# Rows gathered into expert order in the first sixteen blocks, and down weights in 8 KB pieces

## The chip, the cores and the metric

The kernel runs on one core of a Trainium2 chip. The time is the device time of an execution, in microseconds. The engines are TensorE (PE, its weight loads PEld), VectorE (DVE), ScalarE (ACT), GpSimd (POOL) and SyncE (SP, which issues DMAs).

## What is computed

A transformer block over 512 tokens of 1024 columns in float32. Attention and a convolution branch come first; they are not touched except for where their buffers lie. The rest is a mixture of 64 experts:

```python
h = rmsnorm(x, g_ffn)
grp  = argmax(h @ w_rg + b_rg)                       # 1 of 8 groups
top_v, top_j = top_k(le[grp], 2)                     # 2 of 8 experts of the group
wts  = pg_top * softmax(top_v)
y_e  = (silu(h_e @ w_g[e]) * (h_e @ w_u[e])) @ w_d[e]  # rows h_e of the tokens that chose e
x    = rmsnorm(x + sum over both choices of wts * y_e, g_final)
```

Each token has two experts, so there are 1024 rows for 64 experts. An expert has 6 MB of weights: gate and up 1024x512, down 512x1024, in float32.

## The kernel before

The expert stage works in blocks of `BLK` = 64 rows of one expert. The blocks of the first `AHEAD` = 2 experts are blocks 0 and 1; the others are counted at run time (`count_i`, read by every engine as `nblk`; with these inputs 60, 62 blocks in all) and listed in `small_i`, so the loops over blocks are hardware loops.

Weights. The buffer `weights` has 12 places of 1 MB, two sets of six by the block's parity. A set holds gate and up of the first half of the columns (sixths 0, 1), of the second half (2, 3), and down in two halves (4, 5). SP issues a sixth of block b+2 when PE has used that of block b (`gu_used` after each half of gate and up, `down_used` after the block) and when the same sixth of block b+1 has landed (`in_w`), L517 to L525. For gate and up a partition gets 8 KB in one piece; for down two pieces of 4 KB (L476, L485).

Rows. The rows of a block are picked out of `h2` by a product with a one-hot matrix, in every block anew: `gather` (L1378) multiplies, for each of four token tiles, the one-hot of 64 slots with the two halves of `h2`, and sums over the tiles in `ps_rows`. DVE copies them to `rows_sb` (L1120), PE transposes them (`transpose_rows`, L1389), DVE copies them to `hTb` (L1122). The gather for block b+1 stands between the products of block b: tiles 0 and 1 behind the first half of gate and up, tile 2 behind the second half, tile 3 behind the transposes of act, the transposes of rows between the halves of down. DVE makes the one-hot of the next block at the start of a block (L1098 to L1101).

The rest of a block. ACT takes silu of gate (L765), DVE multiplies by up (L1117, `act`), PE transposes act (L1417), ACT copies it (L767), PE multiplies with down (L1426), ACT copies the result to `y_sb` (L773) and GpSimd scatters its rows to `expert_rows` in DRAM (L579). At the end SP reads these rows back (L531), DVE adds them with their weights (L1142) and normalizes.

Before the first block DVE works out the routing in a chain of small operations in which each waits for the one before (`link`); `prepare_slots` (L1061) and `take_slots` (L1075), which list the destination rows of all slots, stand in block 0.

## Time and profile before

| what | us |
|---|---|
| median of 3 runs (1401.35 to 1402.8) | 1401.41 |
| the profiled execution | 1401.0 |
| its span in the trace | 1399.2 |
| PE busy | 1327.6 (95%) |
| DVE busy | 431.9 (31%) |
| ACT busy | 209.4 (15%) |
| GpSimd busy | 186.3 (13%) |
| bytes read from HBM | 429.1 MB |

Times in the views are counted from the start of the span. In the slices of the page each digit is the busy share of 1/40 of the span, 35 us, in tenths. "PEclk" is the clock granted to TensorE. A PE row of the timeline merges instructions of one line; its first number is the start of the first of them, its second reaches to the end of the last, which overlaps the next row. The expert loop fills the span from 430 to 1371 us.

### The profile page before, as it was taken

Reading aid. Unit: us, or ns where it says so; the run is one execution under the profiler, and the core shown is the slowest. Engines: PE = TensorE matmul, PEld = TensorE weight load, DVE = VectorE, ACT = ScalarE, POOL = GpSimd, SP = SyncE. Lnnn points to the kernel's source line nnn. Section 1 sums busy time; section 2 is a strip of 40 time slices with the busy share of each in tenths; the row PEclk is TensorE's granted clock in tenths of the full one; section 3 lists DMA queues with packets and bytes.
Section 4 is the critical chain, followed back from the end, with each engine's and each line's share of the span. In section 5 each row is a group of like instructions: output and inputs, shape, how many; then the busy total and the mean of one; then the engine's idle time right before and its main releaser. Section 6 shows DMA issues by size and latency. Waiting matters only on the chain.

```text
span 1399.2 us, 17476 instructions
## 1 busy us (share of the span) xinstructions
PE 1327.6 (95%) x5883; PEld 580.5 (41%) x5883; DVE 431.9 (31%) x843; ACT 209.4 (15%) x453; POOL 186.3 (13%) x244
## 2 busy tenths in 40 slices
PE   5999988999979999999999999999999999999991
PEld 3878766744453333333333333333333333333330
DVE  4799344342334221121121122122112112112214
ACT  3232324430110100100000000010010000000002
POOL 2355433000000001001001001000100100100100
PEclk9999999999978999999999999999999999999996
DMA  5331311116145999999999999999999999999984
GB/s 208 115 121 61 121 60 57 68 57 251 49 180 219 386 417 416 417 417 417 416 418 417 415 417 417 415 416 417 416 417 417 413 414 410 415 414 415 416 339 186
DMA packets 93090, 435.78 MB, mean 311 GB/s; under 512 B 13488, under 2 KB 13517, under 8 KB 60810
## 3 DMA queue, kind: packets, MB, share of 16 engines
q1 hardware_dynamic: 86896, 429.23, 76.1%
q0 software_dynamic: 5312, 5.28, 1.2%
q10 hardware_dynamic: 858, 0.95, 0.2%
q8 instruction: 15, 0.25, 0.1%
q14 instruction: 9, 0.07, 0.0%
HBM read 429.10 MB, written 18.36 MB: 320 GB/s over the span
## 4 chain that ended last, share of the span: by engine, by line
issue 78%; PE 13%; POOL 2%; DVE 2%; DMA 2%; POOLq 1%; ACT 1%; ACTq 0%; DVEq 0%
PE ps_proj L1193 10%; PE ps_proj L1234 2%; POOL sb_tick L578 1%; POOL sb_tick L589 1%; DVE sb_x L1142 1%; DMA sb_weights<-in_w_in 1%; DMA sb_rb_sb<-in_rel_bias 1%; PE ps_scores L1248 1%; POOL expert_rows L579 0%; DVE sb_x L1152 0%; DVE sb_conv L932 0%; DMA sb_weights<-expert_rows 0%; POOL sb_weights_r L557 0%; PE ps_proj L1216 0%; PE ps_proj L1225 0%
## 5 line engine op out<-in xcount | busy, mean ns | idle before, releaser
L1405 PE MATMUL ps_proj<-sb_weights,sb_scratch 128*64 128x512 f32 x1984 | 446.9, 592 | 0.8 <-DVE sb_scratch L1107 0.8
L1405 PEld LDWEIGHTS ps_proj<-sb_weights,sb_scratch 128*64 128x64 f32 x1984 | 142.3, 137 | 283.2 <-issue 271.8
L1382 PE MATMUL ps_proj<-sb_hT,sb_scratch 128*64 128x512 f32 x1008 | 254.0, 605 | 0.0
L1426 PE MATMUL ps_scores<-sb_weights,sb_scratch 128*64 128x512 f32 x992 | 237.0, 598 | 0.0
L1117 DVE TENSOR_TENSOR sb_scratch<-sb_scratch,ps_proj 128x256 f32<-128x256 f32 x62 | 26.1, 421 | 536.0 <-ACT sb_scratch L765 536.0
L578 POOL TENSOR_TENSOR sb_tick<-sb_tick 1x1 f32<-1x1 f32 x62 | 11.6, 187 | 1013.9 <-ACT sb_scratch L773 1013.9
L1193 PE MATMUL ps_proj<-sb_hT_r,sb_weights_r 128*128 128x512 f32 x512 | 126.9, 401 | 2.7 <-POOL sb_weights_r L557 2.7
L1382 PEld LDWEIGHTS ps_proj<-sb_hT,sb_scratch 128*64 128x64 f32 x1008 | 67.4, 138 | 120.5 <-issue 120.5
L1426 PEld LDWEIGHTS ps_scores<-sb_weights,sb_scratch 128*64 128x64 f32 x992 | 65.3, 136 | 116.9 <-issue 90.3
L1193 PEld LDWEIGHTS ps_proj<-sb_hT_r,sb_weights_r 128*128 128x128 f32 x512 | 96.8, 192 | 30.5 <-issue 10.1
L765 ACT ACTIVATE sb_scratch<-ps_proj 128x256 f32<-128x256 f32 x62 | 23.8, 385 | 492.1 <-PE ps_proj L1405 492.1
L557 POOL TENSOR_TENSOR sb_weights_r<-sb_weights,sb_weights_r 128x1024 fp32r<-128x1024 f32 x36 | 86.0, 2404 | 76.4 <-ACT sb_weights_r L640 75.4
L773 ACT ACTIVATE sb_scratch<-ps_scores 128x512 f32 (+1 forms) x62 | 37.0, 598 | 318.6 <-PE ps_scores L1426 311.0
L1122 DVE COPY sb_scratch<-ps_proj 128x512 f32<-128x512 f32 x62 | 42.9, 692 | 99.5 <-PE ps_proj L1389 99.5
L1120 DVE COPY sb_scratch<-ps_proj 128x512 f32<-128x512 f32 x62 | 42.9, 691 | 96.1 <-PE ps_proj L1382 96.1
L579 POOL DMA_INDIRECT expert_rows<-sb_scratch,sb_idx x62 | 61.4, 991 | 32.3 <-issue 31.9
L1193 PE MATMUL ps_proj<-sb_x_r,sb_weights_r 128*128 128x512 f32 x256 | 63.2, 389 | 0.0
L1341 PE MATMUL ps_proj<-sb_weights 128*128 128x512 f32 x128 | 55.6, 593 | 0.0
L1193 PEld LDWEIGHTS ps_proj<-sb_x_r,sb_weights_r 128*128 128x128 f32 x256 | 48.1, 188 | 10.0
L1389 PEld LDWEIGHTS ps_proj<-sb_consts,sb_scratch 128*128 128x128 f32 x252 | 26.6, 142 | 52.1 <-issue 50.3
L1098 DVE TENSOR_TENSOR sb_scratch<-sb_small,sb_consts 128x512 f32<-128x512 f32 x62 | 43.0, 693 | 7.6 <-issue 1.2
L845 DVE SCALAR_TENSOR_TENSOR ps_scores<-sb_pad,sb_taps,ps_scores 128x512 f32<-128x512 f32 x58 | 42.5, 752 | 0.9
(221 smaller groups left out, 811.1 us busy)
## 6 DMA issues: line engine op xcount, KB each, us to landing
sb_weights<-in_w_exp_down SPq DMA_DIRECT2D x124, 1024.0 KB, 13.8
sb_weights<-in_w_exp_gate SPq DMA_DIRECT2D x124, 1024.0 KB, 14.0
sb_weights<-in_w_exp_up SPq DMA_DIRECT2D x124, 1024.0 KB, 15.2
sb_weights<-in_w_in SPq DMA_DIRECT2D x9, 2048.0 KB, 7.9
sb_x<-in_x SPq DMA_DIRECT2D x8, 512.0 KB, 9.2
sb_weights<-in_w_out SPq DMA_DIRECT2D x2, 2048.0 KB, 10.5
sb_weights<-expert_rows SPq DMA_DIRECT2D x4, 1024.0 KB, 7.9
sb_weights<-in_w_conv_pw SPq DMA_DIRECT2D x1, 2048.0 KB, 7.7
```

Of the source, the lines that this page charges most:

```text
L557: pool.tensor_tensor(w_low[name][:, :, j * P:(j + 1) * P], raw, high.bitcast(F32), ALU.subtract).then_inc(w_split, 1)
L579: pool.indirect_dma_start(out=y_dram, out_offset=bass.IndirectOffsetOnAxis(ap=idx[:, parity:parity + 1], axis=0), in_=y_sb[:, parity, :], ...
L773: act_e.activation(y_sb[:, of_parity(b), :].rearrange("p a s -> p (a s)"), ps_y, ACT.Copy)\
L845: dve.scalar_tensor_tensor(out=dst, in0=pad[:, c, k:k + SEQ], scalar=taps[:, c, k:k + 1], in1=conv_sum[c], op0=ALU.mult, op1=ALU.add).then ...
L1098: dve.tensor_tensor(hot_k, over(dest, BLK), pos8, ALU.is_equal).then_inc(loop_v, 1)
L1120: dve.tensor_copy(rows_sb, ps_rows[:, :]).then_inc(rows_ready, 1)
L1122: dve.tensor_copy(hTb, ps_hTb[:, :].rearrange("p (c s) -> p c s", s=P)).then_inc(hTb_ready, 1)
L1193: last = mm(dst[:, :], w[:, c, :], rows[:, c, :], start=i + c == 0, stop=i == 2 and c == KD - 1)
L1341: last = mm(dst[:, :], gates[:, c, t * P:(t + 1) * P], w[:, c, :], start=c == 0, stop=c == KD - 1)
L1382: last = mm(ps_rows[g * BLK:(g + 1) * BLK, :], onehot[:, t, :], h2[:, t, g * NW:(g + 1) * NW], start=t == 0, stop=t == T - 1)
L1405: last = mm(ps_gu[g * BLK:(g + 1) * BLK, :].rearrange("p (a n) -> p a n", a=2), hTb[:, c, half * BLK:(half + 1) * BLK], weights[:, place(p ...
L1426: last = mm(ps_y[g * BLK:(g + 1) * BLK, :], actT[:, j, half * BLK:(half + 1) * BLK], weights[:, place(parity, 4 + half), 2 * j + g, :], st ...
```

## The change

The rows that a block needs are no longer gathered in every block. 1024 rows fill sixteen blocks of 64, so the rows are gathered sixteen times, in expert order with no gaps, into `hTs`, a buffer that holds them transposed (slot by slot, the eight column chunks of a slot side by side). This is done for the rows of the experts from the third on, beside the blocks 0 to 15; blocks 0 and 1 get their rows as before. Every block from the third on copies its 64 rows from `hTs` to `hTb` (`sorted_to_block`), from a start that DVE reads from `start_i`. `sorted_places`, new on DVE in block 0, works out each row's place and the starts, with two small products on PE (`rest_of_experts`). In the blocks with a gather PE does tiles 2 and 3 between the halves of gate and up, the transposes of rows behind the second half, tile 0 of the next ones behind the transposes of act, tile 1 between the halves of down. Blocks after the sixteenth have no gather and no transposes of rows.

The buffers `v_sb`, `conv`, `strip` and `pad` become parts of one buffer `work`, over which `hTs` and the routing's temporaries lie. A half of down is laid out so that a partition gets two neighbouring rows of the weights, 8 KB in one piece; act is transposed with a stride of two (`act_jf`) to match. The smallest count of loop blocks becomes 16.

```diff
@@ -49,12 +49,15 @@
 BLK = 64
 AHEAD = 2
 MAXB = 80
-MINLOOP = 2 * SEQ // BLK - AHEAD
+MINLOOP = 2 * SEQ // BLK
+GATHERED = 2 * SEQ // BLK - AHEAD
+WORK = 64 + 2 * SEQ * KD + BLK * KD
 NW = 512
 EPS = 1e-6
 LAM_INIT = 0.8 - 0.6 * math.exp(0.0)
 NEG = -3.0e38
 FAR = 1.0e6
...
-        v_sb = sb("v_sb", [P, T, CW])
         scratch = sb("scratch", [P, 4096])
-        pad = sb("pad", [P, KC, SEQ + TAPS - 1])
-        conv = sb("conv", [P, KC, SEQ])
-        strip = sb("strip", [P, HEADS, SEQ])
+        work = sb("work", [P, WORK + 64])
+        v_sb = work[:, 0:2048].rearrange("p (t n) -> p t n", n=CW)
+        conv = work[:, 2048:4096].rearrange("p (c s) -> p c s", s=SEQ)
+        strip = work[:, 4096:6144].rearrange("p (h s) -> p h s", s=SEQ)
+        pad = work[:, 6144:6144 + KC * (SEQ + TAPS - 1)].rearrange("p (c s) -> p c s", s=SEQ + TAPS - 1)
+        hTs = work[:, 128:128 + KD * (2 * SEQ + BLK)]
...
+        act_jf = act.rearrange("p (f j) -> p j f", j=2)
...
-            wd = ap("w_exp_down")[0].rearrange("e (h j p) n -> e h p j n", h=2, p=P)
+            wd = ap("w_exp_down")[0].rearrange("e (h p j) n -> e h p (j n)", h=2, p=P)
...
-                    dst = dst.rearrange("p a (j q) n -> p (a j) (q n)", j=2)
-                    src = wd[e, i - 4].rearrange("e p j n -> (e p) j n")
+                    dst = dst.rearrange("p a b n -> p (a b n)")
+                    src = wd[e, i - 4].rearrange("e p n -> (e p) n")
...
+            def sorted_places():
+                link(dve.tensor_scalar(ecap, const("ahead", NE), float(BLK), ecount, ALU.mult, ALU.min))
+                link(dve.tensor_tensor(erest, ecount, ecap, ALU.subtract))
+                dve.tensor_scalar(erest_b, const("ones", NE), erest, None, ALU.mult).then_inc(rest_ready, 1)
+                link(dve.tensor_tensor(efirst, eend, eblk, ALU.subtract))
+                link(dve.tensor_scalar(efirst, efirst, float(BLK), None, ALU.mult))
+                link(dve.tensor_scalar(starts_m, const("block", NE)[:, 0:MAXB], float(BLK), efirst, ALU.mult, ALU.subtract))
+                link(dve.tensor_scalar(starts_m, starts_m, 0.0, erest, ALU.max, ALU.min))
+                dve.tensor_scalar(starts_m, starts_m, float(KD), None, ALU.mult).then_inc(starts_in, 1)
+                dve.wait_ge(rest_done, 1)
+                link(dve.tensor_copy(cstart, ps_oT[:, 0:NE]))
+                link(dve.tensor_scalar(cstart[:, 0:AHEAD], cstart[:, 0:AHEAD], -float(BLK) - STATIC, None, ALU.add))
+                link(dve.tensor_scalar(over_c, ranks[:, :, 0:AHEAD], float(BLK), STATIC, ALU.is_ge, ALU.mult))
+                link(dve.tensor_tensor(crank, ranks, cstart.unsqueeze(1).to_broadcast([P, T, NE]), ALU.add))
+                link(dve.tensor_tensor(crank[:, :, 0:AHEAD], crank[:, :, 0:AHEAD], over_c, ALU.add))
+                for k in range(2):
+                    link(dve.tensor_tensor(hot_c, hot_e[:, k], crank, ALU.mult))
+                    ins = dve.tensor_reduce(cdest.rearrange("p (t k) -> p t k", k=2)[:, :, k], hot_c, X, ALU.add)
+                    if k == 0:
+                        link(ins)
+                    else:
+                        ins.then_inc(loop_v, 1)
+                dve.wait_ge(starts_done, 1)
+                link(dve.tensor_copy(start_i[0:1, :], ps_t[0:1, 256:256 + MAXB]))
...
+            def block_onehot():
+                dve.wait_ge(loop_v, 2)
+                dve.tensor_tensor(hot_k, over(dest, BLK), pos8, ALU.is_equal).then_inc(loop_v, 1)
+                dve.wait_ge(loop_v, 3)
+                dve.tensor_tensor(onehot, onehot2[:, :, 0, :], onehot2[:, :, 1, :], ALU.add).then_inc(hot_b, 1)
             def next_onehot(before, after):
                 dve.wait_ge(loop_v, before)
...
+                dve.tensor_tensor(hot_k, over(cdest, BLK), pos8, ALU.is_equal).then_inc(loop_v, 1)
                 dve.wait_ge(loop_v, after)
...
+                dve.tensor_scalar(cdest, cdest, -float(BLK), None, ALU.add).then_inc(loop_v, 1)
                 dve.tensor_tensor(onehot, onehot2[:, :, 0, :], onehot2[:, :, 1, :], ALU.add).then_inc(hot_b, 1)
...
+            def copy_rows(n):
+                dve.wait_ge(rows_done, n)
+                dve.tensor_copy(rows_sb, ps_rows[:, :]).then_inc(rows_ready, 1)
+            def rows_to_block(n):
+                dve.wait_ge(hTb_done, n)
+                dve.tensor_copy(hTb, ps_hTb[:, :].rearrange("p (c s) -> p c s", s=P)).then_inc(hTb_ready, 1)
+            def rows_to_sorted(n, at):
+                dve.wait_ge(hTb_done, n)
+                dve.tensor_copy(hTs[:, at].rearrange("p (s g c) -> p c g s", g=2, c=4),
+                                ps_hTb[:, :].rearrange("p (c g s) -> p c g s", c=4, g=2)).then_inc(hTs_ready, 1)
+            def sorted_to_block(start):
+                dve.tensor_copy(hTb.rearrange("p c (g s) -> p c g s", g=2),
+                                hTs[:, bass.ds(start, BLK * KD)].rearrange("p (s g c) -> p c g s", g=2, c=4))\
+                    .then_inc(hTb_ready, 1)
+            def gate_and_up(b):
                 dve.wait_ge(gsig_ready, b + 1)
                 dve.tensor_tensor(act, gsig, ps_gu[:, 256:512], ALU.mult).then_inc(act_ready, 1)
...
+            def list_rows(b, block_slots):
                 if not isinstance(b, int):
                     dve.wait_ge(y_free, b - 1)
                 dve.tensor_copy(idx[:, of_parity(b)], block_slots).then_inc(idx_ready, 1)
...
+            copy_rows(1)
+            rows_to_block(1)
+            dve.wait_ge(rows_done, 1)
+            block_onehot()
+            sorted_places()
+            prepare_slots()
+            gate_and_up(0)
+            copy_rows(2)
+            rows_to_block(2)
+            take_slots()
+            list_rows(0, slots[:, 0:1])
+            def block_with_gather(b, at, start, block_slots):
+                copy_rows(b + 2)
+                next_onehot(2 * b + 4, 2 * b + 5)
+                gate_and_up(b)
+                rows_to_sorted(b + 2, at)
+                dve.wait_ge(hTs_ready, b)
+                sorted_to_block(dve.value_load(start, min_val=0, max_val=2 * SEQ * KD))
+                list_rows(b, block_slots)
+            dve.wait_ge(rows_done, 2)
+            next_onehot(4, 5)
+            block_with_gather(1, slice(0, BLK * KD), start_i[0:1, 0:1], slots[:, 1:2])
             weigh_choices()
             nblk = dve.value_load(count_i[0:1, 0:1], min_val=MINLOOP, max_val=MAXB - AHEAD)
...
+            with dve.Fori(0, GATHERED) as i:
+                block_with_gather(i + AHEAD, bass.ds(BLK * KD * (i + 1), BLK * KD), start_i[0:1, 1:][:, bass.ds(i, 1)],
+                                  slots[:, AHEAD:][:, bass.ds(i, 1)])
+            n = GATHERED + AHEAD
+            copy_rows(n + 2)
+            rows_to_sorted(n + 2, slice(BLK * KD * (n - 1), BLK * KD * n))
+            dve.wait_ge(hTs_ready, n)
+            with dve.Fori(GATHERED, nblk) as i:
+                gate_and_up(i + AHEAD)
+                sorted_to_block(dve.value_load(start_i[0:1, 1:][:, bass.ds(i, 1)], min_val=0, max_val=2 * SEQ * KD))
+                list_rows(i + AHEAD, slots[:, AHEAD:][:, bass.ds(i, 1)])
...
+            def rest_of_experts():
+                pe.wait_ge(rest_ready, 1)
+                mm(ps_oT[:, 0:NE], erest_b, before[0:NE, 0:NE], start=True, stop=True).then_inc(rest_done, 1)
+                pe.wait_ge(starts_in, 1)
+                mm(ps_t[0:1, 256:256 + MAXB], ones[0:NE, 0:1], starts_m, start=True, stop=True).then_inc(starts_done, 1)
+            def gate_up_half(b, parity, half):
+                pe.wait_ge(in_w[2 * half], 16 * b + 16)
+                pe.wait_ge(in_w[2 * half + 1], 16 * b + 16)
+                for c in range(4):
+                    for g in range(2):
+                        last = mm(ps_gu[g * BLK:(g + 1) * BLK, :].rearrange("p (a n) -> p a n", a=2),
+                                  hTb[:, c, half * BLK:(half + 1) * BLK],
+                                  weights[:, place(parity, 2 * half, 2), c, g * 256:(g + 1) * 256],
+                                  start=half + c == 0, stop=half * c == 3)
+                last.then_inc(gu_used, 1)
+            def transpose_act(b):
                 pe.wait_ge(act_ready, b + 1)
                 for c in range(2):
...
+                    last = pe.transpose(ps_actT[:, c * P:(c + 1) * P], act_jf[:, c, :], ident)
                 last.then_inc(actT_done, 1)
...
+            def down_half(b, parity, half):
+                pe.wait_ge(in_w[4 + half], 16 * b + 16)
+                for j in range(2):
+                    for g in range(2):
+                        last = mm(ps_y[g * BLK:(g + 1) * BLK, :], actT[:, j, half * BLK:(half + 1) * BLK],
+                                  weights[:, place(parity, 4 + half), 2 * j + g, :],
+                                  start=half + j == 0, stop=half * j == 1)
+                if half:
+                    last.then_inc(down_used, 1)
+            def first_block():
+                pe.wait_ge(hTb_ready, 1)
+                gate_up_half(0, 0, 0)
+                rest_of_experts()
+                pe.wait_ge(hot_b, 2)
+                gather([0, 1])
+                gate_up_half(0, 0, 1)
+                gather([2])
+                transpose_act(0)
+                gather([3])
+                pe.wait_ge(actT_ready, 1)
+                down_half(0, 0, 0)
+                pe.wait_ge(rows_ready, 2)
+                transpose_rows()
+                down_half(0, 0, 1)
+                slot_rows()
+                pe.wait_ge(hot_b, 3)
+                gather([0, 1])
+            def block_with_gather(b, parity):
+                pe.wait_ge(hTb_ready, b + 1)
+                gate_up_half(b, parity, 0)
+                gather([2, 3])
+                gate_up_half(b, parity, 1)
+                pe.wait_ge(rows_ready, b + 2)
+                transpose_rows()
+                transpose_act(b)
+                pe.wait_ge(hot_b, b + 3)
+                gather([0])
                 pe.wait_ge(actT_ready, b + 1)
...
+                down_half(b, parity, 0)
+                gather([1])
+                down_half(b, parity, 1)
+            def block_products(b, parity):
+                pe.wait_ge(hTb_ready, b + 1)
+                gate_up_half(b, parity, 0)
+                gate_up_half(b, parity, 1)
+                transpose_act(b)
+                pe.wait_ge(actT_ready, b + 1)
+                down_half(b, parity, 0)
+                down_half(b, parity, 1)
+            first_block()
+            block_with_gather(1, 1)
+            with pe.Fori(0, GATHERED // 2) as i:
+                for parity in range(2):
+                    block_with_gather(2 * i + parity + AHEAD, parity)
+            gather([2, 3])
+            pe.wait_ge(rows_ready, GATHERED + AHEAD + 2)
+            transpose_rows()
             pe.wait_ge(listed, 1)
             nblk = pe.value_load(count_i[0:1, 0:1], min_val=MINLOOP, max_val=MAXB - AHEAD)
...
+            with pe.Fori(GATHERED // 2, nblk // 2) as i:
                 for parity in range(2):
                     block_products(2 * i + parity + AHEAD, parity)
             with pe.If((nblk & 1) > 0):
```

## Rows read from the trace of the kernel before

**Rows 1.** Page, part 2: busy tenths of forty slices, granted clock, DMA engines.

```profile
PE   5999988999979999999999999999999999999991
...
PEclk9999999999978999999999999999999999999996
DMA  5331311116145999999999999999999999999984
```

**Rows 2.** Timeline of PE in the loop: start, us, line, operation, count.

```profile
815.80 3.60 PE L1405 MATMUL ps_proj<-sb_weights,sb_scratch 128*64 128x512 f32 x16
819.23 1.03 PE L1382 MATMUL ps_proj<-sb_hT,sb_scratch 128*64 128x512 f32 x4
820.34 0.44 PE L1417 MATMUL ps_aT<-sb_consts,sb_scratch 128*128 128x128 f32 x2
...
821.62 1.89 PE L1426 MATMUL ps_scores<-sb_weights,sb_scratch 128*64 128x512 f32 x8
823.44 0.66 PE L1389 MATMUL ps_proj<-sb_consts,sb_scratch 128*128 128x128 f32 x4
824.03 1.94 PE L1426 MATMUL ps_scores<-sb_weights,sb_scratch 128*64 128x512 f32 x8
```

**Rows 3.** The same timeline of PE in the last block.

```profile
1361.00 3.60 PE L1405 MATMUL ps_proj<-sb_weights,sb_scratch 128*64 128x512 f32 x16
...
1369.22 1.94 PE L1426 MATMUL ps_scores<-sb_weights,sb_scratch 128*64 128x512 f32 x8
```

**Rows 4.** DMA issues of 434.1, 705.0, 780.7, 680 to 695, 1345.1: KB, landing.

```profile
sb_weights<-in_w_exp_gate SPq DMA_DIRECT2D x1, 1024.0 KB, 5.2
...
sb_weights<-in_w_exp_down SPq DMA_DIRECT2D x1, 1024.0 KB, 10.2
...
sb_weights<-in_w_exp_down SPq DMA_DIRECT2D x1, 1024.0 KB, 11.5
...
sb_weights<-in_w_exp_gate SPq DMA_DIRECT2D x2, 1024.0 KB, 11.4
...
sb_weights<-in_w_exp_up SPq DMA_DIRECT2D x1, 1024.0 KB, 15.1
```

**Rows 5.** DMA rates: slices of 700 to 1000; stretches 488:490 and 575:577.

```profile
GB/s 422 414 422 410 421 412 421 412 423 413 418 413 421 411 419 410 424 410 422 411 421 410 419 416 418 414 419 411 422 412 419 414 421 411 418 415 419 416 420 414
...
DMA packets 119, 0.86 MB, mean 430 GB/s; under 512 B 14, under 2 KB 14, under 8 KB 14
...
DMA packets 247, 0.82 MB, mean 408 GB/s; under 512 B 48, under 2 KB 48, under 8 KB 247
```

**Rows 6.** Timeline around the first block: DVE, PE and SP's queue.

```profile
421.66 0.16 DVE L1048 SCALAR_TENSOR_TENSOR sb_conv<-sb_strip,sb_consts 128x2 f32<-128x2 f32 x1
...
424.30 0.42 DVE L1058 TENSOR_REDUCE sb_strip<-sb_conv 128x4 f32<-128x256 f32 x1
...
430.89 0.16 DVE L1064 TENSOR_SCALAR sb_strip<-sb_strip 128x8 f32<-128x8 f32 x1
...
435.54 0.43 DVE L1073 COPY sb_v_sb<-sb_v_sb 128x512 f32<-128x512 f32 x1
439.16 0.42 DVE L1117 TENSOR_TENSOR sb_scratch<-sb_scratch,ps_proj 128x256 f32<-128x256 f32 x1 [3.20 <-ACT sb_scratch L765]
...
445.19 2.01 PE L1375 MATMUL ps_scores<-sb_conv,sb_v_sb 128*128 128x80 f32 x16
447.13 1.08 PE L1405 MATMUL ps_proj<-sb_weights,sb_scratch 128*64 128x512 f32 x4
...
451.34 0.35 SPq L487 DMA_DIRECT2D sb_weights<-in_w_exp_gate  x1
```

**Rows 7.** Timeline of DVE: a strided operation, a copy, and a register load.

```profile
398.02 1.97 DVE L982 SCALAR_TENSOR_TENSOR sb_hT<-sb_x,sb_small,sb_g_ffn 128x1024 f32<-128x1024 f32 x1
...
460.67 0.69 DVE L1122 COPY sb_scratch<-ps_proj 128x512 f32<-128x512 f32 x1 [1.60 <-PE ps_proj L1389]
...
463.57 0.69 DVE L1098 TENSOR_TENSOR sb_scratch<-sb_small,sb_consts 128x512 f32<-128x512 f32 x1 [1.25 <-issue]
```

84 lines of the change are left out of this document (19 added, 65 removed).

## The prediction

> **What bounds the kernel now.** I read the slices of the page first. From the fourteenth slice to the thirty-eighth the PE row is all nines and so is the DMA row [rows 1]: that is the expert loop, 62 blocks, 900 of the 1399 us, with two resources that both look full. A full-looking engine may still be waiting in short pieces, so the next view is the timeline of one block [rows 2]. It shows the order on PE and the starting time of each piece. Half of the gate and up products is 16 products from 815.80 to 819.23, 3.43 us or 0.214 each; a gathered tile is four (0.86), a half of the down products eight (1.71), the transposes of rows take 0.59 (823.44 to 824.03), and those of act with one tile and the wait for their copy 1.28 (820.34 to 821.62), of which 0.05 is wait if the transposes take 0.37. A block has 64 products (13.71), with both kinds of transposes 14.67. From the half that starts at 815.80 to that of the last block at 1361.00 [rows 3] are 36 blocks, so the period is 15.14 and has not moved. The missing 0.47 is four small gaps; the largest, 0.25, stands before the act transposes (819.23 and 0.86 to 820.34). So PE sets the period and hardly ever waits for weights.
>
> The transfers are a hair slower than PE. The time from issue to landing of the first down piece of a block is 10.2 us at 705, 11.5 at 780 (five blocks later); it was 5.2 for the first piece of the loop and is 15.1 for the last up piece [rows 4]. It grows by 0.26 us a block, so the DMA needs 15.14 + 0.26 = 15.40 us for the six pieces of a block while PE needs 15.14, and the lead with which weights land is eaten up. At the end the last up piece is issued at 1345.1 and lands 15.1 later, at 1360.2 [rows 4]; the products that read it start at 1361.00 [rows 3]. PE and DMA reach the end within 1 us of each other. That is the key to this case: take all gathering from PE in 46 of 62 blocks and the DMA stream, whose end does not move for it, takes over at once.
>
> **The gather leaves 46 blocks.** A block then costs PE 3.43 + 3.43 for gate and up, 1.11 until the act transposes (819.23 to 820.34), 1.28 from them to the first down product (820.34 to 821.62; part of that is a gathered tile, so this is an upper value), 3.43 for down: 12.7 us at most against 15.4 of DMA [rows 2]. PE has 2.7 us to spare a block, and 62 x 6 MB still have to come. What this alone gives is the end: after the last up piece lands (1360.2), PE needs 3.43 + 1.11 + 1.28 + 3.43 = 9.25 us, so it ends the products at 1369.4; before, the last half of down starts at 1369.22 and ends 1.71 later, at 1370.93 [rows 3]. Gain 1.5 us. The two down pieces land behind it at 2.6 us each (15.4 for six), before their products come, and are not waited for.
>
> **Down weights as 8 KB pieces.** Two stretches of 2 us hold one size of piece alone: with 8 KB 430 GB/s, with 4 KB 408 [rows 5]. The 2.1 MB of down of a block take 4.88 us at the one rate and 5.14 at the other, 0.26 apart. The row of forty slices of 7.5 us between 700 and 1000 alternates, since a slice is half a block: the slices without down average 420.6 GB/s, those with it 412.2. Down pieces fill about 0.68 of the latter, so they run at 408.2, and 2.1 MB take 5.137 instead of 4.986 us: 0.15 a block [rows 5]. I take 0.15, because that row averages 20 blocks and the two stretches only 2 us each; the bounds are 0.26 above and 0 below (if the slices with down are slower for the row scatters in them). The permutation of rows of act (a transposed operand of stride two) has no row; 0 to 0.1 us on PE, hidden in the late blocks by the 2.7. The new layout of buffers and the clearing of 512 columns on GpSimd stand at the start, where no row shows a wait for GpSimd's first work; I cost them at nothing.
>
> The Trainium skill (DMA: Bandwidth & Descriptors, Specifications) puts the smallest transfer for line rate at 512 B. By it the merged piece brings 0; the two stretches above speak against it, with 430 against 408 GB/s.
>
> **The first block.** The change puts `sorted_places` on DVE between the one-hot and `prepare_slots`, and holds PE for its two products. In the rows of before, the one-hot is just over when `prepare_slots` begins at 430.89; it runs to 435.97, 5.08 us [rows 6]; nothing waits for it, since gate-times-up comes only at 439.16. The new function is about 8 small operations of 0.2 to 0.28 each to the two signals (2.0 us, to 432.9), then a wait for the first product. PE is at its own first half until 433.33; the product is 64 columns and I allow 0.6 with its signal (an estimate from the 0.214 of a product of 512, and the 0.21 to 0.27 by which DVE and ACT follow a last product in these rows), so DVE goes on at 434.06. What follows has the same operations as L1048 to L1058, which took 421.66 to 424.72, 3.06 us, and two small ones: 3.4, to 437.45. With `prepare_slots` 442.5; gate-times-up is ready at 442.97 instead of 439.58 (439.16 and 0.42). PE is 1.0 us late by the two products, then idles from 440.4 to 443.0, transposes, gathers, and ends the first down at 448.4 (before: just ahead of 445.19). The slot product takes 1.94 (445.19 to 447.13), to 450.4, and the new wait for the third one-hot stands behind `take_slots` on DVE: 0.6 us of slots, 0.15 of idx, 1.3 of one-hot, 452.45. Then two tiles (1.72) are gathered ahead. The second block starts at 454.2 instead of 447.13 [rows 6]: 7.1 us later, and every release to SP with it.
>
> Does this reach the DMA? SP issues the next gate piece at 451.34 after that release [rows 6]; transfers at the loop's start take 5.2 from issue to landing, with the queue empty [rows 4], less than the 7.1 by which it is late. So yes, nearly in full. Following the pieces one by one with 5.2 us as the least time to landing, an idle queue lands the first new gate piece at 463.8 and two blocks later the stream is 6.2 us behind before (5.2 to 7.5). Before, the queue was itself waiting a little here, which absorbs the difference.
>
> **The blocks with a gather.** The same 64 products and transposes stand in the block (14.67 us), but the transposes of rows now fill the wait for act instead of a gathered tile: the gap there is 1.11 - 0.59 = 0.52 instead of 0.25, others 0.1: 15.30. That is no more than the DMA needs (15.40, or 15.25 with 8 KB), so the stream keeps its lag. On DVE two copies take the place of one. A copy of 128x512 is 0.69; written or read with stride eight it may be 1.5 times that, 1.06, since L982, which reads with stride eight, takes 1.97 for 1024 elements [rows 7]. A register load costs DVE 1.25, the idle time before L1098 at 463.57 [rows 7]. After act: 1.06 + 1.25 + 1.06 = 3.4 us, while PE has 0.37 + 0.91 + 1.71 + 0.86 + 1.71 = 5.6 until the next block. Hidden, with 2.2 to spare.
>
> **Leaving the gather.** After the sixteenth block PE does two tiles (1.72), waits for the copy (0.27 + 0.69), transposes (0.59), and reads the count (part of 1.25): about 4 us. PE has the weights by then, but SP does not get its release. The start of block 17 is 7.1 + 15 x 0.16 + 4 = 13.5 us behind before; a queue with little in it lands the pieces 5.2 after issue, where gate pieces of before had 11.4 by then [rows 4]. So the stream is 13.5 + 5.2 - 11.4 = 7.3 behind; 6.2 if the queue still has work, 9 if the wait is longer. I take 7.3.
>
> **The sum.** Start and leaving +7.3 (the 6.2 of the start are in it); end -1.5; 44 blocks' pieces at 8 KB in the bound part, 44 x 0.15 = -6.6 (in the gathering blocks the faster pieces only shorten the queue, PE's 15.30 holds there). Sum -0.8: span 1398.4 beside 1399.2. The profiled execution took 1401.0 in all and the median of the runs is 1401.41, 0.4 more, so the time is 1401.4 - 0.8 = 1400.6.
>
> **The rivals.**
> (1) The small packets cost their upper bound and the leaving is covered: 6.2 - 1.5 - 44 x 0.26 = -6.7: 1394.7. For it: 430 against 408 GB/s; against: the slice row.
> (2) The merged piece is not faster, because what slows the slices with down is the scatter of rows that falls in them. Then 7.3 - 1.5 = +5.8: 1407.2. For it: the 2% between the slices could hide such traffic; against: the 2 us with 4 KB pieces alone [rows 5].
> The rule of 512 B on the Trainium skill's page DMA: Bandwidth & Descriptors (Specifications) would give this case.
> (3) On the other side also: the new DVE chain decides in the gathering blocks. The next block's first product waits for `sorted_to_block`; the point is 5.6 us after act. If strided copies take three times a plain one (2.1 each), the chain is 5.5 and PE stands at the edge; a chain of 6.6 adds 1 us to each of 15 blocks, 15 in all, since the DMA is then short of releases: 1400.6 + 15 = 1415.6. Against: the ratio of rows 7, by which 2.2 us are to spare.
> (4) TensorE's clock. It stood at full speed (2.4 GHz) in every slice of the loop, and fell in the two slices around 420 us, where the PE row shows idle time [rows 1]. The late blocks leave PE idle for some 2.7 us of 15.4, in two or three pieces. If the clock fell to 1.2 GHz and stayed, the 48 products of a block would take 10.3 us more, 23.0, and 40 blocks 40 x 7.6 = 304 us more: 1705. A fall in one stretch hides in the 2.7.
> The Trainium skill (TensorE: Matmul & The Clock Gate, HAM oscillation) warns of idle gaps between bursts that halve the clock; the trace agrees for the routing stretch, and no row of before shows gaps as short and as many as these.
>
> **Chances.** Forecast 0.43 (own range 1397 to 1404.5), (1) 0.27, (2) 0.15, (3) 0.12, (4) 0.03. A measurement of this kernel can tell about 0.2%, 2.8 us. Of the forecast 0.05 lies faster than that and 0.05 slower. Faster 0.32, same 0.33 and slower 0.35. The range goes from (1) to (2): 1393.5 to 1407.5; (3) and (4) are left out.
>
> **What would show it.** In the trace after: second block's first product near 454; blocks with gather every 15.3 us with the gap before the act transposes at 0.5; from the seventeenth block some six blocks of 12.7, then PE waits for gate and up pieces, and the block's period is the DMA's, 15.25; packets of 4 KB gone but for scatters, slices all near 420 GB/s; PE clock 1.00. The last product near 1370. Wrong if the gathering blocks differ from 15.3 by over 0.3, if the late period is 15.4 or under 15.1, or if the stream at block 20 is not 6 to 9 us behind.

## The result, and the profile after

The changed kernel takes 1406.55 us in the median (1404.45 to 1408.16), the one before 1401.54 (1398.58 to 1403.35) in runs beside it: 1.0032 of it, interval 1.0023 to 1.0042. It is slower by 5 us, 0.3%. The profiled execution took 1406.4, its span 1404.3 beside 1399.2, so 5.1 us have to be found in the trace.

The page of the changed kernel: span, PE's busy time, the slices, and from the groups of instructions the gate and up products.

```profile
span 1404.3 us, 15645 instructions
...
PE 1166.5 (83%) x4987; PEld 532.8 (38%) x4987; DVE 363.0 (26%) x697; ACT 209.4 (15%) x453; POOL 186.5 (13%) x245
...
PE   5999988999978999999989777777777777777771
...
PEclk9999999999968999999999999999999999999996
DMA  5331311116044899999999999999999999999984
GB/s 207 114 121 60 121 60 59 71 51 261 39 180 182 320 406 419 418 410 416 406 420 420 419 420 419 420 419 420 420 420 419 420 420 420 415 418 419 419 360 188
DMA packets 77219, 435.79 MB, mean 310 GB/s; under 512 B 13488, under 2 KB 13517, under 8 KB 29066
...
L1489 PE MATMUL ps_proj<-sb_weights,sb_scratch 128*64 128x512 f32 x1984 | 449.9, 595 | 96.1 <-DMA sb_weights<-in_w_exp_up 94.6
```

PE is busy for 161 us less than before and its gate and up products wait 96 us in all, 94.6 of them for up pieces: from the twenty-third slice its digit is 7, DMA's stays 9, and the clock stays at full speed; in [rows 1] PE and DMA both showed nines up to the end. The work did leave PE and the bound did move to the stream. Why the time rose all the same is in three places: the first block, the moment where the gather ends, and the rate of the stream behind it.

The first block, timeline of PE in the changed kernel (start, us, line, operation, count, and in brackets the idle time before it and what ended it):

```profile
439.82 1.03 PE L1462 MATMUL ps_proj<-sb_hT,sb_scratch 128*64 128x512 f32 x4
443.26 0.51 PE L1498 MATMUL ps_aT<-sb_consts,sb_scratch 128*128 128x128 f32 x2 [2.41 <-DVE sb_scratch L1168]
443.70 1.29 PE L1462 MATMUL ps_proj<-sb_hT,sb_scratch 128*64 128x512 f32 x4
444.77 3.42 PE L1505 MATMUL ps_scores<-sb_weights,sb_scratch 128*64 128x512 f32 x8
...
448.71 1.94 PE L1505 MATMUL ps_scores<-sb_weights,sb_scratch 128*64 128x512 f32 x8
450.58 2.01 PE L1455 MATMUL ps_scores<-sb_work 128*128 128x80 f32 x16
454.60 3.63 PE L1462 MATMUL ps_proj<-sb_hT,sb_scratch 128*64 128x512 f32 x8 [2.01 <-DVE sb_scratch L1146]
458.02 3.64 PE L1489 MATMUL ps_proj<-sb_weights,sb_scratch 128*64 128x512 f32 x16
```

And the windows of the same stretch (length, busy time and instructions of each engine, granted clock, DMA):

```profile
440.40:443.80 3.40, 0.99 (x8) 0.42 (x6) 2.71 (x5) 0.03 (x1) 0.00 (x0) 1.00 1.00 359
443.80:447.20 3.40, 3.40 (x10) 0.95 (x12) 0.69 (x1) 0.38 (x1) 0.00 (x0) 0.59 0.91 383
447.20:454.00 6.80, 5.39 (x32) 2.77 (x28) 2.00 (x5) 0.51 (x1) 0.00 (x0) 0.95 0.27 92
454.00:457.40 3.40, 2.80 (x8) 0.97 (x10) 0.51 (x3) 0.08 (x1) 1.51 (x2) 0.60 1.00 422
```

The second block starts at 458.02, 10.9 us later than at 447.13 [rows 6]. The two waits for DVE stand where they were expected (2.41 and 2.01 us idle). Behind each, the granted clock is 0.59 and 0.60 in the mean, so for the most part at the lower of its levels, 1.2 instead of 2.4 GHz: the eight down products at 444.77 take 3.42 instead of 1.89 us, the eight of the gather at 454.60 take 3.63 instead of 1.89. From start to start the three groups at 443.70, 444.77 and 454.60 cost 0.16, 1.53 and 1.71 more than at full clock (1.07 beside 0.91, 3.35 beside 1.82, 3.42 beside 1.71), 3.4 us in all.

A block with a gather, the last of them, and a late block, again PE:

```profile
565.37 3.60 PE L1489 MATMUL ps_proj<-sb_weights,sb_scratch 128*64 128x512 f32 x16
...
575.07 0.51 PE L1498 MATMUL ps_aT<-sb_consts,sb_scratch 128*128 128x128 f32 x2 [0.35 <-DVE sb_scratch L1168]
...
690.72 0.66 PE L1469 MATMUL ps_proj<-sb_consts,sb_scratch 128*128 128x128 f32 x4 [0.79 <-DVE sb_scratch L1150]
692.00 7.09 PE L1489 MATMUL ps_proj<-sb_weights,sb_scratch 128*64 128x512 f32 x32 [0.62 <-issue]
700.02 0.50 PE L1498 MATMUL ps_aT<-sb_consts,sb_scratch 128*128 128x128 f32 x2 [0.93 <-DVE sb_scratch L1168]
...
785.64 3.65 PE L1489 MATMUL ps_proj<-sb_weights,sb_scratch 128*64 128x512 f32 x16 [1.33 <-DMA sb_weights<-in_w_exp_up]
...
1366.94 3.65 PE L1489 MATMUL ps_proj<-sb_weights,sb_scratch 128*64 128x512 f32 x16 [1.34 <-DMA sb_weights<-in_w_exp_up]
```

Up to the sixteenth block the period is 15.33 (458.02 to 565.37 are seven). From 785.64 to 1366.94 are 38 blocks of 15.30 in the mean, in which PE waits for up pieces. The timeline of SP's queue gives two issues, and the DMA view of each its landing:

```profile
696.19 0.34 SPq L498 DMA_DIRECT2D sb_weights<-in_w_exp_gate  x1
...
sb_weights<-in_w_exp_gate SPq DMA_DIRECT2D x1, 1024.0 KB, 5.1
```

```profile
1351.84 0.34 SPq L498 DMA_DIRECT2D sb_weights<-in_w_exp_up  x1
...
sb_weights<-in_w_exp_up SPq DMA_DIRECT2D x1, 1024.0 KB, 15.0
```

The first is the gate piece that goes out when the gather has ended: it lands at 701.3. The same piece of the kernel before was issued at 678.50 and landed 11.3 later, at 689.8. The stream is 11.5 us behind. It was 11.2 behind already before the gather ended: the gate piece of one block earlier was issued at 676.85 and landed 9.1 later, before at 663.35 and 11.4 later. The last up piece lands at 1366.8; before, at 1360.2 [rows 4]. There it is 6.6 behind. So the stream wins back 4.9 us over 43 blocks, 0.11 a block. After the last up piece the span has 37.5 us left, before 39.0 (1399.2 - 1360.2): 1.5 won at the end. 11.5 - 4.9 - 1.5 = 5.1. The profile accounts for all of the loss; what the 11.5 are made of was put to the chip.

### The profile page after: what moved, and what is told of

Read it like the earlier page. It is cut to its first block, busy times and chain, and to the rows that moved or that the text cites. A ratio compares the mean times of both kernels' runs of the same rounds, so it can differ in the third digit from the quotient of the medians.

```text
span 1404.3 us, 15645 instructions
## 1 busy us (share of the span) xinstructions
PE 1166.5 (83%) x4987; PEld 532.8 (38%) x4987; DVE 363.0 (26%) x697; ACT 209.4 (15%) x453; POOL 186.5 (13%) x245
## 4 chain that ended last, share of the span: by engine, by line
issue 78%; PE 13%; POOL 2%; DVE 2%; DMA 2%; POOLq 1%; ACT 1%; ACTq 0%; DVEq 0%
PE ps_proj L1273 10%; PE ps_proj L1314 2%; POOL sb_tick L590 1%; POOL sb_tick L601 1%; DVE sb_x L1222 1%; DMA sb_rb_sb<-in_rel_bias 1%; DMA sb_weights<-in_w_in 1%; PE ps_scores L1328 1%; POOL expert_rows L591 0%; DVE sb_x L1232 0%; DVE sb_work L944 0%; DMA sb_weights<-expert_rows 0%; POOL sb_weights_r L569 0%; PE ps_proj L1296 0%; PE ps_proj L1305 0%
## 5 line engine op out<-in xcount | busy, mean ns | idle before, releaser
L1489 PE MATMUL ps_proj<-sb_weights,sb_scratch 128*64 128x512 f32 x1984 | 449.9, 595 | 96.1 <-DMA sb_weights<-in_w_exp_up 94.6
L1489 PEld LDWEIGHTS ps_proj<-sb_weights,sb_scratch 128*64 128x64 f32 x1984 | 151.9, 137 | 387.3 <-issue 386.0
L1505 PE MATMUL ps_scores<-sb_weights,sb_scratch 128*64 128x512 f32 x992 | 230.0, 600 | 21.8 <-ACT sb_scratch L779 21.8
L1462 PE MATMUL ps_proj<-sb_hT,sb_scratch 128*64 128x512 f32 x288 | 76.1, 634 | 2.0 <-DVE sb_scratch L1146 2.0
L1498 PE MATMUL ps_aT<-sb_consts,sb_scratch 128*128 128x128 f32 x124 | 31.4, 335 | 50.6 <-DVE sb_scratch L1168 50.6
L1498 PEld LDWEIGHTS ps_aT<-sb_consts,sb_scratch 128*128 128x128 f32 x124 | 19.6, 207 | 95.5 <-DVE sb_scratch L1168 95.5
L1150 DVE COPY sb_scratch<-ps_proj 128x512 f32<-128x512 f32 x18 | 12.5, 692 | 136.1 <-PE ps_proj L1462 136.1
L1162 DVE COPY sb_scratch<-sb_work 128x512 f32 x61 | 38.1, 624 | 32.2 <-issue 20.2
L857 DVE SCALAR_TENSOR_TENSOR ps_scores<-sb_work,sb_taps,ps_scores 128x512 f32<-128x512 f32 x58 | 42.6, 753 | 0.9
L1421 PEld LDWEIGHTS ps_proj<-sb_weights 128*128 128x128 f32 x128 | 24.2, 190 | 29.8 <-issue 29.7
## 6 DMA issues: line engine op xcount, KB each, us to landing
sb_weights<-in_w_out SPq DMA_DIRECT2D x2, 2048.0 KB, 10.3
```

The lines of the kernel that those rows point to most:

```text
L857: dve.scalar_tensor_tensor(out=dst, in0=pad[:, c, k:k + SEQ], scalar=taps[:, c, k:k + 1], in1=conv_sum[c], op0=ALU.mult, op1=ALU.add).then ...
L1162: dve.tensor_copy(hTb.rearrange("p c (g s) -> p c g s", g=2), hTs[:, bass.ds(start, BLK * KD)].rearrange("p (s g c) -> p c g s", g=2, c=4))\
L1421: last = mm(dst[:, :], gates[:, c, t * P:(t + 1) * P], w[:, c, :], start=c == 0, stop=c == KD - 1)
L1462: last = mm(ps_rows[g * BLK:(g + 1) * BLK, :], onehot[:, t, :], h2[:, t, g * NW:(g + 1) * NW], start=t == 0, stop=t == T - 1)
L1489: last = mm(ps_gu[g * BLK:(g + 1) * BLK, :].rearrange("p (a n) -> p a n", a=2), hTb[:, c, half * BLK:(half + 1) * BLK], weights[:, place(p ...
L1498: last = pe.transpose(ps_actT[:, c * P:(c + 1) * P], act_jf[:, c, :], ident)
```

## The experiments

**Eight-KB pieces alone.** The kernel before with the new layout of down and the transposes of act that match it:

```diff
-            wd = ap("w_exp_down")[0].rearrange("e (h j p) n -> e h p j n", h=2, p=P)
+            wd = ap("w_exp_down")[0].rearrange("e (h p j) n -> e h p (j n)", h=2, p=P)
-                    last = pe.transpose(ps_actT[:, c * P:(c + 1) * P], act[:, c * P:(c + 1) * P], ident)
+                    last = pe.transpose(ps_actT[:, c * P:(c + 1) * P], act_jf[:, c, :], ident)
```

> The kernel before with down weights as one 8 KB piece a partition, gather as it was. Theory A (the down pieces shorten the DMA's block by 0.1 us and PE sets the block's period at 15.14): no change in time, within 1 us of the kernel before; the time to landing grows by 0.15 us a block instead of 0.26, and every block still takes 15.14. Rival (the pieces cost or bring time by themselves): 4 us or more either way.

It took 1404.95 us (1401.05 to 1406.67), 1.0024 of the kernel before (1.0012 to 1.0035): slower by 3.4. Groups of instructions of the kernel before and of this one, the transposes of act and their weight loads:

```profile
L1417 PE MATMUL ps_aT<-sb_consts,sb_scratch 128*128 128x128 f32 x124 | 27.2, 301 | 5.1
...
L1417 PEld LDWEIGHTS ps_aT<-sb_consts,sb_scratch 128*128 128x128 f32 x124 | 12.5, 140 | 59.7 <-DVE sb_scratch L1117 59.7
```

```profile
L1418 PE MATMUL ps_aT<-sb_consts,sb_scratch 128*128 128x128 f32 x124 | 31.3, 334 | 5.0
...
L1418 PEld LDWEIGHTS ps_aT<-sb_consts,sb_scratch 128*128 128x128 f32 x124 | 19.5, 206 | 59.6 <-DVE sb_scratch L1118 59.6
```

The loaded operand with a stride of two takes 206 instead of 140 ns, the product behind it 334 instead of 301. Two of them make 0.07 us a block, and every block of this kernel takes 15.21 instead of 15.14. Over 61 blocks that is 4.3, and its span is 3.8 longer than before. The pieces do land faster: the last down piece at 1359.1 beside 1365.6, 6.5 us earlier, about 0.1 a block, as the stream wins in the changed kernel. But PE sets the period here, so the gain is invisible and the cost is not. That "no change" was expected is a miss: the layout has a price on PE, and only a stream-bound block hides it.

**The same with the permutation on DVE.** Gate-times-up reads its inputs in order and writes act in the order that plain transposes need, each pair of neighbours 128 elements apart:

```diff
-                dve.tensor_tensor(act, gsig, ps_gu[:, 256:512], ALU.mult).then_inc(act_ready, 1)
+                dve.tensor_tensor(act.rearrange("p (j f) -> p f j", j=2), gsig.rearrange("p (f j) -> p f j", j=2),
+                                  ps_gu[:, 256:512].rearrange("p (f j) -> p f j", j=2), ALU.mult).then_inc(act_ready, 1)
```

> The kernel before with 8 KB down pieces, where act is permuted by DVE's write (stride 128) instead of by PE's transposes (stride two). Theory A (the transposes of act with stride two take PE 0.07 us longer in each of 62 blocks, 15.21 instead of 15.14, and this is the 3 to 4 us by which the 8 KB pieces alone were slower): block 15.14, time as the kernel before, within 1 us. Rival (the loss is in the transfers): 1404.9 as with the strided transposes.

1412.33 us (1407.79 to 1413.9), ratio 1.0076 (1.005 to 1.0101). Groups of instructions, DVE's multiplication and the transposes:

```profile
L1117 DVE TENSOR_TENSOR sb_scratch<-sb_scratch,ps_proj 128x256 f32<-128x256 f32 x62 | 37.3, 602 | 536.0 <-ACT sb_scratch L765 536.0
...
L1418 PE MATMUL ps_aT<-sb_consts,sb_scratch 128*128 128x128 f32 x124 | 27.2, 301 | 16.3 <-DVE sb_scratch L1117 16.3
```

The transposes are back at 301 ns, but the multiplication takes 0.60 instead of 0.42 and PE waits for it: 15.32 a block. The price moved from 0.07 on PE to 0.18 on DVE, still on the path. Both expectations, the time of the kernel before and 1404.9, were missed.

**Four-KB pieces put back into the changed kernel**, with the plain transposes (the first diff the other way round).

> The changed kernel with down weights again in two pieces of 4 KB. Theory A (from the sixteenth block on the DMA stream sets the time, and 8 KB pieces save 0.11 us in each of 44 blocks): 5 us longer than the changed kernel, 1411.5, late blocks every 15.4 us. Rival (the piece size is of no use, the 0.11 is something else): 1406.5, within 1.5 us.

1411.86 us (1410.18 to 1414.02), ratio 1.0069 (1.0052 to 1.0085): 5.3 above the changed kernel, as expected. The gathering blocks take 15.26 instead of 15.33 (the transposes again), most late blocks 15.40 instead of 15.29. From the windows behind 850 us, one (DMA's share and GB/s are the last two columns):

```profile
850.00:1000.00 150.00, 112.47 (x496) 37.45 (x494) 11.05 (x30) 13.64 (x30) 13.53 (x30) 1.00 1.02 416
```

416 beside 419 to 420 GB/s is 0.8%, 0.12 us of a block. So in the changed kernel the merged pieces are worth 5.3 us of 1400, and without them it would be slower by almost 10. The Trainium skill (DMA: Bandwidth & Descriptors, Specifications) has 512 B as the smallest transfer for line rate; the pieces of both kernels are far above it, and these two still differ by that 0.8%. The measurement decides: here the size still matters.

**Keep PE busy in the two waits.** If the 3.4 us are the clock's, products without use in the waits should bring them back. First with five and four of them:

```diff
                 gather([2])
+                for _ in range(5):
+                    mm(ps_y, ident, h2[:, 0, 0:NW], start=True, stop=True)
                 transpose_act(0)
...
                 slot_rows()
+                for _ in range(4):
+                    mm(ps_gu[:, :], ident, h2[:, 0, 0:NW], start=True, stop=True)
                 pe.wait_ge(hot_b, 3)
```

> The changed kernel with nine products whose results nobody reads put into the two waits of PE in the first block (2.4 us before the act transposes, 2.0 us before the gather at its end). The waits stay, only PE isn't idle in them. Theory A (PE's idling makes the clock fall, and twice 3.4 us at half clock put the start back by 3.4 us, which the stream carries to the end): second block 3.4 us earlier, clock 1.00 throughout, 1403.1. Rival (the clock's fall is hidden behind transfers, the loss is the waits alone): 1406.5.

1407.72 us (1405.79 to 1408.93), ratio 1.0039 (1.0024 to 1.0053). It came nearer to the rival's 1406.5 than to the expected 1403.1, but it decides nothing. A product with the 128 columns of the identity loaded took 0.88 us, twice one of the gather's, so the fillers were 4.4 and 3.6 us long and overran waits of 2.4 and 2.0. The clock stayed up and the overrun ate what it gave. With two and two of them:

> As the kernel with nine filling products, but two in each of the two waits of PE in the first block: a filling product takes 0.88 us, as the nine showed, so two fill 1.75 us of the 2.4 and 2.1 us of waiting and delay nothing. Theory A (the idle time makes the clock fall, and the two falls put the start back by 3.4 us): from the first block's gate and up products to those of the second 27.6 - 3.4 = 24.2 us, clock 1.00 over both, time 3.4 us below the changed kernel, 1403.1. Rival (what the waits cost is in the waits alone): 1406.5.

1402.83 us (1397.59 to 1405.74), ratio 1.0009 (0.9995 to 1.0024). Its timeline of PE, and its windows:

```profile
440.65 1.98 PE L1520 MATMUL ps_scores<-sb_hT,sb_consts 128*128 128x512 f32 x4
443.13 0.51 PE L1498 MATMUL ps_aT<-sb_consts,sb_scratch 128*128 128x128 f32 x2 [0.50 <-DVE sb_scratch L1168]
443.57 1.08 PE L1462 MATMUL ps_proj<-sb_hT,sb_scratch 128*64 128x512 f32 x4
444.48 1.89 PE L1505 MATMUL ps_scores<-sb_weights,sb_scratch 128*64 128x512 f32 x8
...
454.54 3.60 PE L1489 MATMUL ps_proj<-sb_weights,sb_scratch 128*64 128x512 f32 x16
```

```profile
444.00:447.40 3.40, 3.40 (x20) 1.22 (x18) 1.10 (x2) 0.06 (x1) 0.00 (x0) 1.00 0.81 340
...
454.00:457.40 3.40, 3.40 (x18) 1.15 (x16) 0.00 (x0) 0.00 (x0) 0.21 (x1) 1.00 0.58 240
```

The transposes start where they did (443.13 beside 443.26), so DVE's chain is as late as ever; but the down products take 1.89, the second block starts at 454.54 instead of 458.02, and the time is 3.7 below the changed kernel's. The fillers compute nothing that is used. The clock's part of the loss is shown, and that it goes to the end: 3.4 us in the first block, 3.6 in the span.

**A stall in the kernel before.** Does an idle PE alone lower the clock, and is a delay of the first block carried to the end where PE is the bound? Plain copies on DVE in block 0:

```diff
                 dve.wait_ge(gsig_ready, b + 1)
+                if isinstance(b, int) and b == 0:
+                    for _ in range(3):
+                        link(dve.tensor_copy(ge[:, :, 0:BLK], pos8))
```

> The kernel before with three copies of 128x512 on DVE (some 0.7 us each) ahead of gate-times-up in the first block, nothing else changed; PE waits 2.2 us longer there. Theory A (a delay of the first block reaches the end one to one, for neither PE nor the DMA stream can make it up, and the clock falls after a wait of that length): 2.2 us, and 1.7 more if the clock falls, so 1403.6 to 1405.5 beside 1401.5. Rival (the slack between PE and DMA takes up a delay of this size): 1401.5, within 0.5 us.

1402.49 us (1399.49 to 1404.55), ratio 1.0009 (0.9994 to 1.0023). The copies took 0.43 each, PE idled only 1.47 us ahead of the transposes, and the clock did not fall: the stall cost 1.4, under what the times can tell. So this run left the question open; with six copies:

> The kernel before, with six plain copies of 128x512 in series on DVE ahead of gate-times-up in the first block only. In the run with three of them each took 0.43 us and the first block became 1.4 us longer, with no fall of the clock. With six PE idles some 2.5 to 2.9 us ahead of the transposes of act, as long as the 2.41 that it idles there in the changed kernel. Theory A (an idle of that length drops the clock for the next 3.4 us, and every delay of the first block goes to the end one to one): the distance between the silu of blocks 0 and 1 grows from 17.23 by 2.7 + 1.7 = 4.4, the half of down ahead of which it stands takes 3.4 instead of 1.89, and the time is 1401.6 + 4.4 = 1406.0. Theory B (the clock does not fall for such an idle alone; in the changed kernel it fell for what else PE had done before): distance +2.7, down at 1.89, time 1404.3. If the time is within 1 us of before, delays of the first block are not carried to the end in the kernel before.

1405.76 us (1400.83 to 1407.81), ratio 1.0026 (1.0013 to 1.0039). Timeline and windows:

```profile
442.48 0.44 PE L1420 MATMUL ps_aT<-sb_consts,sb_scratch 128*128 128x128 f32 x2 [2.85 <-DVE sb_scratch L1120]
442.84 1.83 PE L1385 MATMUL ps_proj<-sb_hT,sb_scratch 128*64 128x512 f32 x4
444.45 2.88 PE L1429 MATMUL ps_scores<-sb_weights,sb_scratch 128*64 128x512 f32 x8
```

```profile
439.60:443.00 3.40, 0.55 (x6) 0.36 (x6) 2.62 (x7) 0.05 (x1) 0.00 (x0) 1.00 0.99 378
443.00:446.40 3.40, 3.40 (x10) 1.01 (x10) 0.69 (x1) 0.34 (x1) 0.00 (x0) 0.51 0.93 369
```

Idle for 2.85 us, then half clock: the gathered tile takes 1.61 from start to start instead of 0.91, down 2.82 instead of 1.82. The distance of the silu of blocks 0 and 1 grows from 17.23 to 21.70, by 4.5 (4.4 expected), and every one of the next sixty silus is 4.5 later than before. The median rose by 3.7 and the span by 4.8. In this execution one added wait of 2.8 us cost 1.7 more through the clock, and nothing of it was won back in 62 blocks. Three of the twelve executions (1400.83, 1401.71 and 1402.12) are as fast as the kernel before; their mean granted clock is 0.979 to 0.980 against 0.974 to 0.976 in the others. They have no trace, so whether the clock stayed up in the first block or somewhere ahead of it is not known.

**Without most of the gather.** A quarter of the gather's products in each of the fifteen blocks and none behind the first block, so three quarters of the gathered sum are left out; DVE's work is unchanged:

```diff
                 pe.wait_ge(hot_b, 3)
-                gather([0, 1])
...
-                gather([2, 3])
+                thin([2, 3])
...
-                gather([0])
...
-                gather([1])
```

> The changed kernel with two of the sixteen gather products in every block from the second on (one token tile alone; the rows that the experts get are not the right ones: the computation leaves out three quarters of the gather), and without the gather at the end of the first block. The stages and waits stay. Theory A (after the start the DMA stream sets the time also in the gathering blocks, the loss is that of the first block): 1.7 us at the start is won, 0.5 us at most in the gathering blocks, so 1404.0 to 1405.0. Rival (the gathering blocks at 15.33 us and the leaving cost 4 us): 1402 or less.

1402.18 us (1397.55 to 1402.91), ratio 1.0006 (0.9993 to 1.0019): 4.4 below the changed kernel, where 1404.0 to 1405.0 was expected if the first block held the loss and 1402 or less if the gathering blocks and the leaving did. The gathering blocks fell to 13.33 until the stream bound them at 15.29 by the tenth, so 2 us of each left PE. The clock fell twice here too. Behind the second wait stands now the second block:

```profile
450.70 5.35 PE L1489 MATMUL ps_proj<-sb_weights,sb_scratch 128*64 128x512 f32 x16 [2.00 <-DVE sb_scratch L1146]
455.88 1.03 PE L1532 MATMUL ps_proj<-sb_hT,sb_scratch 128*64 128x512 f32 x4
```

Its first sixteen products take 5.18 us from start to start; in the changed kernel they take 3.48 (458.02 to 461.50). So the half clock was not avoided, it moved from the gathered tiles to gate and up, and at the start only the 1.7 us were won that the two tiles take at full clock. The rest of the 4.4, 2.7 us by the medians, is in the gathering blocks and the leaving. The profiled execution says the same less exactly, because it was the fastest of the ten and early already before the expert loop: its span is 8.9 shorter than that of the changed kernel, 3.9 of it ahead of the act transposes of the first block (439.37 beside 443.26) and 1.7 at the first block's end, which leaves 3.3. So the first block isn't the only place that holds time: without most of the gather some 3 us more could be had. How they divide between the fifteen blocks and the leaving is open.

**The first block in another order.** All work of `sorted_places` is kept, but DVE does only its first half before `prepare_slots` and the rest while PE is in down; PE's two small products stand ahead of the transposes of act, and the gather of tiles 0 and 1 moves into block 1:

```diff
-            sorted_places()
+            first_places()
             prepare_slots()
             gate_and_up(0)
+            ranks_of_rest()
             copy_rows(2)
+            places_of_rest()
             rows_to_block(2)
+            next_onehot(4, 5)
             take_slots()
...
                 gate_up_half(0, 0, 0)
-                rest_of_experts()
...
                 gather([2])
+                rest_of_experts()
                 transpose_act(0)
...
                 slot_rows()
-                pe.wait_ge(hot_b, 3)
-                gather([0, 1])
```

> The changed kernel with the first block in another order: DVE does gate-times-up before the second part of the places, the two small products of PE stand before the act transposes, the first two tiles of the next rows are gathered in the second block and not before it. Theory A (the whole loss is the first block's 11 us, carried to the end by the DMA stream): second block starts 0.5 to 1 us behind the kernel before instead of 11, the clock stays at 1.00, the stream is some 3 us behind (1.7 us of gather are made up for in the second block) instead of 11.2, so 8 us are gained: 1398.5, below the kernel before. Rival (the blocks with a gather, at 15.33 us instead of 15.14, and the leaving cost 4 us or more by themselves): 1402.5 or more.

1399.49 us (1397.87 to 1400.31), ratio 0.998 (0.9969 to 0.9991). This beats both kernels, by 2.6 and by 7.1. The timeline of PE:

```profile
441.50 0.43 PE L1486 MATMUL ps_oT<-sb_consts,sb_work 64*128 64x64 f32 x2
...
442.09 0.51 PE L1504 MATMUL ps_aT<-sb_consts,sb_scratch 128*128 128x128 f32 x2
...
443.44 1.89 PE L1511 MATMUL ps_scores<-sb_weights,sb_scratch 128*64 128x512 f32 x8
...
449.65 3.65 PE L1495 MATMUL ps_proj<-sb_weights,sb_scratch 128*64 128x512 f32 x16
```

No bracket, no idle time, the clock at 1.00. The second block starts at 449.65; its routing was 2.0 us later in this execution, so that is 0.5 more than before, and 2.2 with the gather of tiles 0 and 1 that block 1 now has to do, where the changed kernel pays 10.3. From there on it is the changed kernel: 15.33 a block with a gather, then the stream at 15.29.

**The same order with 4 KB pieces and plain transposes.**

> The changed kernel with the reordered first block, and with down in 4 KB pieces and act transposed plainly, as before. Theory A (the late blocks are bound by the DMA stream at 15.29 us a block with 8 KB pieces and 15.40 with 4 KB; all else is PE's start): the order of the first block and the size of the pieces are independent terms, so this kernel is 5 above the reordered one, as 4 KB pieces were 5.3 above the changed kernel: 1399.5 + 5 = 1404.5, and it is slower than before although it starts early: gathering blocks 15.26, late blocks 12.4 for a few and then 15.40. Theory B (with the early start the stream has slack, so the size matters less): within 2 us of the reordered kernel, 1401.5 or less.

1404.63 us (1400.19 to 1406.35), ratio 1.0019 (1.0008 to 1.003): 5.1 above the reordered kernel (5 expected). The order of the first block (7.1 us) and the size of the pieces (5.1 to 5.3) are two terms that add. In eight blocks between the 25th and the 34th its period was 15.09 to 15.14 instead of 15.40. The kernels with 8 KB pieces have such a stretch there too (15.01 to 15.05 in the reordered one, from the 25th to the 29th); I have no cause for it.

## Why the prediction was wrong

Forecast: 1400.6, no change that can be told. Measured: 1406.55, slower by 0.3%. That is close to the 1407.2 of rival (2), by coincidence: its mechanism, merged pieces without effect, is refuted below. The 0.35 that the forecast gave to "slower" lay mostly on rivals that did not occur.

- **What bounds the kernel.** Right: before, PE, with the stream only just slower than it; after, the stream alone. The first five late blocks took 12.44 us each (12.7 forecast as an upper value), the later ones the stream's 15.30 (15.25).
- **The first block's order.** Right to 0.3 us. Last copy of `prepare_slots` done and gate-times-up started at 442.80 (forecast 442.5 for the end, act ready 442.97, measured 443.21); transposes at 443.26 (443.0); slot product at 450.58 where 448.4 was forecast, because of the clock. Without the 3.4 us of clock and the 0.6 by which the routing ended later in this execution the second block is 6.9 late; 7.1 was forecast. (DVE's start behind the first product was put at 434.06, 0.13 more than its own terms, 433.33 and 0.6, give; measured 434.51, or 433.96 without those 0.6.)
- **The clock. This is the step that failed.** Rival (4) looked for idle time in the late blocks alone, and said that a fall in one stretch would be hidden there. The timeline that the forecast itself drew had PE idle from 440.4 to 443.0 and again until the third one-hot, in a block where nothing hides a loss. Its sum had no term for the clock there. The late blocks, with PE idle in pieces of at most 1.4 us, kept 1.00. It cost 3.4 us, shown by the short fillers. The Trainium skill (TensorE: Matmul & The Clock Gate, HAM oscillation) was cited for gaps between bursts that halve the clock. Here every idle time of 2.0 us or more in the first block was followed by the fall (2.41, 2.01, 2.85) and none of 1.5 or less was (1.47, and 1.36 and 0.93 in the late blocks). The trace of the kernel before already held such idle times ahead of its expert loop. Its timeline of PE and its windows show one with the fall and one without:

```profile
25.76 3.91 PE L1193 MATMUL ps_proj<-sb_hT_r,sb_weights_r 128*128 128x512 f32 x16 [2.67 <-POOL sb_weights_r L557]
...
400.05 1.97 PE L1318 MATMUL ps_proj<-sb_consts,sb_hT 128*128 128x128 f32 x8 [1.94 <-DVE sb_hT L982]
```

```profile
26.00:28.00 2.00, 2.00 (x10) 1.61 (x10) 0.00 (x0) 1.44 (x2) 0.30 (x1) 1.00 0.00 0
...
400.00:402.00 2.00, 1.96 (x10) 1.96 (x10) 0.69 (x1) 0.00 (x0) 0.00 (x0) 0.50 1.00 418
```

It fell behind 3.79, 3.52 and 2.98 us too (202.73, 242.36 and 276.53). So a price for an idle time of 2 us could have been read before the change, and also that it is not paid every time: behind 2.67 us at 25.76 the clock stayed at 1.00, and in the profiled execution with the thinned gather it stayed there behind the 2.98 (278.79) and the 1.93 (400.64), which is why that execution was early. What decides it is not shown.
- **Does the delay reach the stream.** Forecast: 6.2 of 7.1, the difference absorbed by a queue that waited anyway. Measured: all of it. The first gate piece behind the first block was issued 10.9 late (462.21 beside 451.34 [rows 6]) and landed 9.4 late, 462.21 + 5.1 beside 451.34 + 6.6, but two blocks on the gate piece landed 11.3 late (492.87 + 9.1 beside 481.62 + 9.1). What the queue gave it took back, since the issues of both kernels go by PE's releases. The stall of six copies shows the same without the change: 4.5 in, 4.5 out.
- **Gathering blocks.** 15.33 (15.30). The copies with stride eight took 1.09 us (1.06), and PE never waited for them (DVE's work after act ended 2.5 us behind it, 3.4 forecast): rival (3) fell.
- **Leaving.** The second block started at 458.02 and fifteen of 15.33 go to 687.98; the seventeenth starts at 692.00, 4.0 later, as forecast. In the kernel before that start lay at 447.13 + 15 x 15.14 = 674.23, so it is 17.8 late where 13.5 was forecast, and SP's gate piece 17.7. By the forecast's own formula (start + 5.2 - 11.4) this gives 11.5, which is what was measured. The term was +7.3 and measures +11.5: 3.4 of the difference is the clock, 0.6 the routing, 0.2 the rest.
- **The size of pieces.** Right in kind, too large: 0.15 a block forecast, 0.11 measured, 4.9 instead of 6.6. The forecast took all of the difference between slices with and without down for the pieces' size; by what was won, a quarter of that difference was something else; what, no run shows. (The row averages 420.5 and 412.5, not 420.6 and 412.2, which makes the forecast's 0.15 a 0.14.) Rival (2), no effect, is refuted by the two kernels with 4 KB put back (5.3 and 5.1 us); rival (1) had more than twice the measured effect.
- **The strided transposes.** Forecast 0 to 0.1 and hidden; 0.07, and hidden in the late blocks but not in the sixteen of the gather, where it adds up to 1.1 us. The forecast's 15.30 had no term for them; without them these blocks take 15.26, as in the kernel with 4 KB put back.
- **The end.** -1.5 forecast, -1.5 measured.

With measured terms the forecast's sum is 11.5 - 4.9 - 1.5 = +5.1 in place of 7.3 - 6.6 - 1.5 = -0.8. The 5.9 between the two are 3.4 of clock, 1.7 of the pieces' size, 0.6 of routing and 0.2 of the rest. The pieces alone would have left the sum at +0.9 and the clock alone at +2.6, both under the 2.8 that the forecast held for measurable; the clock is the larger of the two, and it takes both for the answer "slower".
